# Prompt attention of a hybrid decoder step: normalization moved behind the value products

## The reference

```python
s = einsum('bqgrd,bngd->bqgrn', q, ck) * scale - slopes * dist_c
p = softmax(where(vm, s, NEG)) * vm
o_cmp = einsum('bqgrn,bngd->bqgrd', p, cv)
...
s2 = einsum('bqgrd,bqgnd->bqgrn', q, ks) * scale - slopes * dist_s
p2 = softmax(where(m2, s2, NEG))
o_slc = einsum('bqgrn,bqgnd->bqgrd', p2, vs)
# o_win: the same with the window branch's keys and values
g = sigmoid(gates)
o = g[..., 0:1] * o_cmp + g[..., 1:2] * o_slc + g[..., 2:3] * o_win
```

## Time and profile before

| | |
|---|---|
| three runs, us | 3301.79, 3307.1, 3315.38 (median 3307.1) |
| the profiled execution, span | 3315.7 us |
| PE busy | 3062.8 us (92%) |
| DVE busy | 2161.3 us (65%) |
| ACT busy | 1199.0 us (36%) |
| POOL busy | 522.0 us (16%) |

### The profile page before, as it was taken

The page is one execution under the profiler, slowest core; times in us unless marked ns, Lnnn a source line. Parts: engine busy times, 40 slices in busy tenths (PEclk is TensorE's granted clock), DMA queues, the critical chain, the costliest instruction groups (busy, mean ns, idle before and its releaser), DMA issues.

```text
span 3315.7 us, 57097 instructions
## 1 busy us (share of the span) xinstructions
PE 3062.8 (92%) x23903; PEld 2911.4 (88%) x23903; DVE 2161.3 (65%) x3361; ACT 1199.0 (36%) x2108; POOL 522.0 (16%) x294
## 2 busy tenths in 40 slices
PE   7999999997988877999898899999999999999995
PEld 7999988996867655788897899999999999999995
DVE  3111777815645444366556888888888889888887
ACT  2000333104634332244223444444444444444342
POOL 2333332433460020011232000000000000000000
PEclk6999999998999987899998999999999999999997
DMA  6744245418812166022633434444444447344332
GB/s 195 224 123 126 70 131 156 139 52 279 282 66 110 71 249 190 17 89 83 169 87 93 140 116 123 122 122 123 125 126 126 126 126 237 120 144 162 97 111 105
DMA packets 517928, 443.70 MB, mean 134 GB/s; under 512 B 33168, under 2 KB 469552, under 8 KB 510750
## 3 DMA queue, kind: packets, MB, share of 16 engines
q1 hardware_dynamic: 453608, 306.83, 31.8%
q0 software_dynamic: 17488, 75.78, 6.1%
q10 hardware_dynamic: 46576, 57.44, 5.1%
HBM read 377.39 MB, written 70.93 MB: 135 GB/s over the span
## 4 chain that ended last, share of the span: by engine, by line
PE 43%; DVE 6%; DMA 1%; issue 1%; ACT 1%; ACTq 0%; DVEq 0%; SPq 0%
PE i L2537 37%; PE i L129 6%; DMA x_blocks<-s_blk 1%; DVE x_blocks L3041 1%; DVE f_half L3003 1%; DVE y_rows L3113 0%; DVE ln_parts L3047 0%; DVE y_rows L3118 0%; DVE resid L2902 0%; ACT x_blocks L2818 0%; DVE x_blocks L2916 0%; DMA x_rows<-s_h 0%; PE i L2546 0%; DVE m_lo L2849 0%; DVE h_rows L3036 0%
## 5 line engine op out<-in xcount | busy, mean ns | idle before, releaser
L2537 PE MATMUL i<-x_blocks,f_half 128*128 128x272 f32 x10752 | 1368.2, 289 | 36.6 <-DVE h_rows L3036 13.7
L2537 PEld LDWEIGHTS i<-x_blocks,f_half 128*128 128x128 f32 x10752 | 1359.4, 190 | 41.3 <-DVE x_blocks L3041 16.0
L2752 ACT CAST f_half<-w_ring 128x1024 fp32r<-128x1024 f32 (+2 forms) x370 | 346.2, 936 | 408.2 <-PE i L2537 355.5
L3003 DVE TENSOR_TENSOR f_half<-w_ring,f_half 128x1024 fp32r<-128x1024 f32 (+2 forms) x362 | 393.1, 1086 | 81.2 <-ACT f_half L2752 78.4
L129 PE MATMUL a<-x_hi,w_hi 128*128 128x272 f32 x1664 | 349.5, 291 | 18.3 <-POOL w_lo L545 18.3
L129 PE MATMUL a<-x_hi,w_lo 128*128 128x272 f32 x1664 | 345.9, 289 | 0.0
L129 PE MATMUL a<-x_lo,w_hi 128*128 128x272 f32 x1664 | 344.8, 289 | 0.0
L545 POOL TENSOR_TENSOR w_lo<-w_ring,w_hi 128x2048 fp32r<-128x2048 f32 x52 | 240.8, 4631 | 455.6 <-DVE w_hi L553 455.6
L129 PEld LDWEIGHTS a<-x_hi,w_hi 128*128 128x128 f32 x1664 | 263.5, 189 | 23.7 <-POOL w_lo L545 23.0
L129 PEld LDWEIGHTS a<-x_lo,w_hi 128*128 128x128 f32 x1664 | 263.2, 190 | 0.0
L553 DVE CAST w_hi<-w_ring 128x2048 fp32r<-128x2048 f32 x52 | 70.7, 1362 | 293.7 <-PE a L129 293.7
(11 more groups left out here) (498 smaller groups left out, 4585.8 us busy)
## 6 DMA issues: line engine op xcount, KB each, us to landing
w_ring<-in_ffn_w_up_dram SPq DMA_DIRECT2D x88, 1024.0 KB, 10.6
w_ring<-in_w_in_dram SPq DMA_DIRECT2D x52, 1024.0 KB, 6.9
w_ring<-in_ffn_w_down_dram SPq DMA_DIRECT2D x24, 1536.0 KB, 7.9
w_ring<-in_w_o_dram SPq DMA_DIRECT2D x16, 1024.0 KB, 6.0
x_blocks<-s_blk ACTq DMA_DIRECT2D x17, 816.0 KB, 5.8
s_blk<-x_sums ACTq DMA_DIRECT2D x22, 544.0 KB, 6.8
s_proj<-x_nat ACTq DMA_DIRECT2D x40, 272.0 KB, 2.6
kv_ring<-in_cmp_w_dram SPq DMA_DIRECT2D x16, 512.0 KB, 11.6
```

The lines of the kernel that those rows point to most:

```text
L2537: last = nc.tensor.matmul(ps[bank][:, 0:HT2], half(e, j, wl_)[:, s], XB[:, x0 + s, xl_, BLK_OF[j]], start=start and s == 0 and i == 0, sto ...
L2752: nc.scalar.copy(half(e, j, 0), source(e, j)).then_inc(hq, 1)
L3003: nc.vector.tensor_tensor(half(e, j, 1), source(e, j), half(e, j, 0).bitcast(F32), ALU.subtract).then_inc(lv, 1)
```

## The change

The softmax weights are no longer normalized before the value products. `turn` transposes the bare exponentials with the identity as operand (a plain transpose, one record), and `values` exchanges its operands, so that the queries stand on the partitions of the result; the three branches go to three separate column ranges of the bank. DVE then combines them (`combine`): reciprocal of the sums, times the gates, and three 128x128 steps that read the bank and add the branches with their factors. The row result is transposed back by PE (`out_turn`), and ACT copies it to `mix` for each job.

The compressed branch of all heads is done once, in front: 32 small score products, bias, shift by the maximum, one exponential, normalization, four transposes. Its weights lie on 64 partitions (8 heads x 8 blocks), and the compressed values `CVX` are laid out so that a head's product picks its own rows (other heads' rows are zero). For this the stage before makes the hidden rows for four heads (`HIDX`, four activations) and one masked 64x1024 product on DVE. All queries are loaded at once to `MIX` in the stage before, in place of two heads there and six loads in the attention; each head's result then overwrites its queries.

The core of the diff:

```diff
-                for h in range(2):
-                    sp.dma_start(Q[:, h], S_proj[h * P:(h + 1) * P, 0:SEQ]).then_inc(q_in[h], 16)
+                sp.dma_start(MIX[:, 0:H, 0:SEQ], S_proj[0:H * P, 0:SEQ].rearrange("(h p) n -> p h n", p=P)).then_inc(q_in, 16)
...
-                nc.vector.tensor_copy(CVP[:].rearrange("p g d -> p (g d)"), ps[2][0:NPB, 0:KVH * HD]).then_inc(ckv, 1)
+                dve.wait_ge(kv_in, 144)
+                nc.vector.tensor_tensor(CVX, ps[2][0:H * NPB, 0:HD].rearrange("p (o d) -> p o d", o=1).broadcast_to((H * NPB, H, HD)),
+                                        OWN.rearrange("p (h o) -> p h o", o=1).broadcast_to((H * NPB, H, HD)), ALU.mult).then_inc(ckv, 1)
...
+                def compressed_scores():
+                    for t in range(QT):
+                        for h in range(H):
+                            at = (t * H + h) * NPB
+                            last = nc.tensor.matmul(pso[1][:, at:at + NPB], MIX[:, h, t * P:(t + 1) * P], CKP[:, :, h // GRP], start=True, stop=True)
+                    last.then_inc(c_scores, 1)
...
                     for br in range(2):
-                        u = UNITS[j] + br
-                        pe.wait_ge(d_ready, u + 1)
+                        u = 2 * j + br
+                        pe.wait_ge(e_ready, u + 1)
                         if u >= 2:
                             pe.wait_ge(pts_ready, u - 1)
                         for k in range(qt + 1):
-                            last = nc.tensor.matmul(pst[u % 2][:, k * P:(k + 1) * P], SC[:, j % 3, br, k * P:(k + 1) * P], DG[:, j % 2, br],
-                                                    start=True, stop=True)
+                            last = nc.tensor.transpose(pst[u % 2][:, k * P:(k + 1) * P], SC[:, j % 3, br, k * P:(k + 1) * P], ident)
...
-                    nc.tensor.matmul(o, CVP[:, g], PTC[:, h % 2, qt * P:(qt + 1) * P], start=True, stop=False)
+                    nc.tensor.matmul(o[:, 0:HD], PTC[:, qt * P:(qt + 1) * P], CVX[:, h], start=True, stop=True)
                     for br in range(2):
-                        pe.wait_ge(pts_ready, UNITS[j] + br + 1)
+                        pe.wait_ge(pts_ready, 2 * j + br + 1)
                         for k in range(qt + 1):
-                            last = nc.tensor.matmul(o, V[:, k, br, g], PTS[:, j % 2, br, k * P:(k + 1) * P], start=False, stop=br == 1 and k == qt)
+                            last = nc.tensor.matmul(o[:, (br + 1) * HD:(br + 2) * HD], PTS[:, j % 2, br, k * P:(k + 1) * P], V[:, k, br, h // GRP],
+                                                    start=k == 0, stop=k == qt)
...
+                def out_turn(j):
+                    pe.wait_ge(r_ready, j + 1)
+                    nc.tensor.transpose(pso[j % 2][:, 0:HD], OR[:, j % 2], ident).then_inc(ot_done, 1)
...
                 scores(1)
+                compressed_scores()
                 for j in range(NJ):
                     turn(j)
                     if j + 2 < NJ:
                         scores(j + 2)
+                    if j == 1:
+                        compressed_turn()
                     if j:
                         values(j - 1)
+                    if j >= 2:
+                        out_turn(j - 2)
...
+                def combine(j):
                     h, qt = JOBS[j]
+                    o, r, to = pso[j % 2], RI[:, j % 2], OR[:, j % 2]
+                    dve.wait_ge(e_ready, 2 * j + 2)
+                    ch.link(nc.vector.reciprocal(r, SU[:, j % 4]))
+                    ch.link(nc.vector.tensor_tensor(r, r, GAB[:, qt, 3 * h + 1:3 * h + 3], ALU.mult))
+                    dve.wait_ge(o_done, j + 1)
+                    if j >= 2:
+                        dve.wait_ge(ot_done, j - 1)
+                    ch.link(nc.vector.tensor_scalar(to, o[:, HD:2 * HD], r[:, 0:1], None, ALU.mult))
+                    ch.link(nc.vector.scalar_tensor_tensor(to, o[:, 2 * HD:3 * HD], r[:, 1:2], to, ALU.mult, ALU.add))
+                    nc.vector.tensor_tensor(to, o[:, 0:HD], to, ALU.add).then_inc(r_ready, 1)
```

More of the change, by code:

```diff
@@ L47 @@
 BIG = 1e33
+NPB_ = SEQ // BLK
 R_Q, R_KV, R_QKV = 0, O_KV, O_GATE
@@ L705, in build @@
         kv_in = sem("a_kv_in")
-        q_in = [sem(f"a_q_in{i}") for i in range(2)]
+        q_in = sem("a_q_in")
         att = ExitStack()
@@ L827, in _ @@
                 nc.tensor.matmul(ps[0][:, :], W2[:, 0], HID[:, 0], start=True, stop=True).then_inc(out4, 1)
[L828 to L831, removed]
+                nc.tensor.matmul(ps[1][:, 0:2 * NPB], W2[:, 0], HIDP[:], start=True, stop=True).then_inc(out4, 1)
+                nc.tensor.matmul(ps[2][0:H * NPB, 0:HD], HIDX[:].rearrange("p g r n -> p (g r n)"), W2[:, 1], start=True, stop=True).then_inc(out4, 1)
                 for k in range(4):
@@ L862, in _ @@
                 act.wait_ge(pc, 1)
-                for c in range(2):
-                    nc.scalar.activation(HIDP[:, c], ps[6 + c][:, 256:256 + 2 * NPB], ACT.Silu).then_inc(hid, 1)
+                nc.scalar.activation(HIDP[:], ps[6][:, 256:256 + 2 * NPB], ACT.Silu).then_inc(hid, 1)
+                for r in range(GRP):
+                    last = nc.scalar.activation(HIDX[:, :, r], ps[7][:, 256:256 + 2 * NPB].rearrange("p (n g) -> p g n", g=KVH), ACT.Silu)
+                last.then_inc(hid, 1)
             @block.vector
@@ L1060, in _ @@
                         scores(j + 2)
+                    if j == 1:
+                        compressed_turn()
                     if j:
                         values(j - 1)
+                    if j >= 2:
+                        out_turn(j - 2)
                 values(NJ - 1)
+                for j in range(NJ - 2, NJ):
+                    out_turn(j)
             @block.scalar
@@ L1093, in output @@
                     h, qt = JOBS[j]
-                    if qt == QT - 1:
-                        act.wait_ge(o_done, QT * (h + 1))
-                        nc.scalar.copy(MIX[:, h, 0:SEQ], pso[h % 2][:, :]).then_inc(o_out, 1)
+                    act.wait_ge(ot_done, j + 1)
+                    nc.scalar.copy(MIX[:, h, qt * P:(qt + 1) * P], pso[j % 2][:, 0:HD]).then_inc(o_out, 1)
                 for j in range(NJ):
                     expo(j)
+                    if j == 0:
+                        act.wait_ge(c_shift, 1)
+                        c = SCC[:].rearrange("p t h n -> p (t h n)")
+                        nc.scalar.activation(c, c, ACT.Exp).then_inc(c_exp, 1)
                     if j >= 1:
                         turned(j - 1)
+                    if j == 1:
+                        act.wait_ge(c_turned, 1)
+                        nc.scalar.copy(PTC[:], pso[0][0:H * NPB, :]).then_inc(c_ready, 1)
                     if j >= 3:
                         output(j - 3)
+                output(NJ - 3)
                 turned(NJ - 1)
-                output(NJ - 3)
-                output(NJ - 2)
-                output(NJ - 1)
+                for j in range(NJ - 2, NJ):
+                    output(j)
             @block.vector
@@ L1112, in _, with by_block, compressed_bias @@
                 ch = Count(dve, ch5)
[L1114 to L1117 removed]
+                def by_block(x):
+                    return x.rearrange("p t (h o) -> p t h o", o=1).broadcast_to((P, QT, H, NPB))
+                def compressed_bias():
+                    for h in range(H):
+                        last = nc.vector.tensor_scalar(BC[:, :, h], cp("dist_c").rearrange("p (t n) -> p t n", t=QT), cp("slope")[:, h:h + 1], None, ALU.mult)
+                    ch.link(last)
```

160 lines of the change are left out of this document (65 added, 95 removed).

## The result

| | before | after |
|---|---|---|
| runs, us | 3301.79, 3307.1, 3313.75, 3315.38 | 3270.86, 3272.02, 3277.91, 3282.89 |
| median, us | 3310.43 | 3274.97 |
| profiled execution, span, us | 3315.7 | 3276.0 |
| attention stage in it, us | 173.75 | 138.82 |
| one head in it, us | 19.87 | 14.74 |

The changed kernel is faster by 1%: ratio 0.9897, interval 0.9879 to 0.9915. The forecast of 3277 is 2 us from the median. The stage, from PE's first product of the attention to its first one of the next stage, lost 34.9 us where 30.2 were forecast.

What follows compares the result with a forecast made beforehand. PE's waits for DVE's diagonal matrices in a multi-engine loop were taken as the bound. Stage: 0.4 + 9.5 + 8 x 15.4 + 3.5, plus 7.0 for the long head, 143.6 against 173.8 us, -30: 3277 us, range 3262 to 3295.

Steps and rivals of the forecast that it cites:

- PE's work in a head: PE's products and transposes for one attention head: 17.41 us before, 14.9 after, bounds 14.1 to 16.9.
- The loop: Tightest at the four-key-tile job: 4.6 us from scores to turn, PE busy 4.05, waiting 0.5; a head 15.4 us.
- The output of job a: DVE's combination for the one-key-tile job: done at 3.9 us, PE arrives at 3.65 to 3.85; nothing counted.
- DVE: DVE's combination costs 1.4 us a job; 12.5 us of work in a head of 15.4, so it hides.
- The front: Start of the attention stage, compressed scores of all heads first: costs 9.5 us, bounds 8 and 9.5 + 5.
- The tail: Last values, combination, transpose and copy of the final job behind the loop: 3.5 us over a whole head.
- The long head: One attention head, coinciding with the gather of the sample group's rows, stays 7.0 us longer than usual.
- The rival in which it vanishes: The 7.0 us stall of one attention head falls elsewhere or on nothing: another -7, 3270 us; chance 0.25.
- Neighbours: Stage before the attention: about +0.4 us from extra activations; the 2 MB query load nothing, at most +3.
- Turns that don't get cheaper: Rival: a transpose in the turns costs 0.23 us like a product, 16.9 us a head, 3289 us; chance 0.07.
- DVE as the bound: Rival: DVE sets the head at 16.6 to 17.2 us, 12 us more, 3289 us; chance 0.08.
- the fallen clock in the loop: Rival: attention stage stays at 1.2 GHz through front pauses and transposes, 98 us more, 3375 us; chance 0.03.

Runs made afterwards that it cites:

- the kernels built from the one before: Kernel before, normalization left out: plain transposes with the diagonal wait kept, 3300.55 us; identity products without that wait, 3288.98; transposes without it, 3271.3.
- the doubled step: Changed kernel with the first of DVE's three output steps of each job made twice: 3275.61 us, heads of 14.74.
- the kernel with all three edits: Changed kernel with 128-row compressed value product, job 1 ahead of the compressed branch in front, ACT's copies ahead of exponentials: 3260.53 us, ratio 0.9868.
- three close relatives of it: Changed kernel with ACT's copies ahead of exponentials, 3273.72 us; with job 1 ahead of the compressed branch, 3261.8; with both and 128-row compressed value products, 3260.53.
- the first kernel: Changed kernel with the turns as full products with the identity in place of plain transposes: 3291.38 us, heads of 16.38.
- the third form of the kernel before: Kernel before without diagonals and normalization, turns as plain transposes waiting for the exponentials alone: 3271.3 us, heads of 15.40.
- the last edits: Changed kernel with ACT's copies ahead of the exponentials, 3273.72 us; with that, 128-row compressed value products and job 1 first in front, 3260.53.

## Why the prediction was right, point by point

- *PE's work in a head* was forecast as 14.9, and a wait of 0.5 beside it. Measured are 14.26 and 0.48 (by starts 13.89 and 0.85). The term that was mis-sized is the transpose: 0.131 from the busy time of 48 in another stage, where eight take 0.91, start to start, 0.113 each. Twenty make 0.36 us less. The output transposes are 0.11, not 0.2, another 0.36. Together they are nearly the difference of a head, 15.4 to 14.74: 0.66 x 8 = 5.3 us of the stage.
- *The loop.* The place (job d), the partner (ACT), and the chain (4.64 against 4.6) came as laid out. That the wait has the forecast size (0.48 against 0.5) is in part luck: it is two waits, 0.31 for ACT and 0.17 for DVE, and by starts PE is late by 0.85, since it needs 3.79 us beside the chain and not 4.05. The output of job a, called tight, is late by 0.17 and costs nothing, as counted, since that time lies beside the chain.
- *Wait and transposes apart.* "Turns now wait for ACT's exponentials and no diagonals" is worth 2.7 us a head and the transposes 1.8, by the kernels built from the one before.
- *DVE* needs 1.45 us a job for the five steps of the combination (1052.38 to 1053.83), forecast 1.4. It hides, as the doubled step shows, even at a busy share of 88%; but the room at job a is only some 0.5 us (0.38 and 0.15), and the kernel with all three edits has used it up.
- *The front* costs 11.16 us (22.07 to the first turn of d, less 10.91 for the same piece of a steady head), forecast 9.5. The step that failed is "All compressed scores come first: 8 x 0.88 = 7.0 us": they took 8.7, since the clock fell to 0.50 before they ended. The prediction took the fall of the earlier trace rows for the result of idle time and expected the load to prevent it; PE was busy 5.00 of 5 us and the mean clock was 0.67. All eight kernels that make these scores first had the clock fall during them.
- *The tail* costs 4.66 against 3.5: its last value product, combination and transpose stand one behind the other with waits of 0.36, 1.10 and 0.90 us.
- *The long head* shrank to 5.14 where 7.0 were kept. Of the 1.9, 1.0 is a shorter pause (3.5 against 4.5) and 0.9 a shorter stretch at the low clock behind it. The rival in which it vanishes did not occur in the changed kernel, but in three close relatives of it, if those can be compared (see above): it is better priced as a spread of 0 to 7 us than as a case of its own.
- *Neighbours.* The stage started 0.26 us later (forecast 0.4), and the query load of 2 MB cost nothing.
- *The sum:* 11.16 + 8 x 14.74 + 5.14 + 4.66 = 138.9, and 138.82 is measured. The forecast counted from the same start 143.2. Its errors of +1.7 in the front, -5.3 in the heads, -1.9 in the long head and +1.2 in the tail make -4.3. That the whole time came within 2 us is in part luck. The forecast took 30.2 from 3307.1, the median of three runs; with the fourth run that median is 3310.43, and the gain is 35.5. An error of 3.3 in the one and of 5.3 in the other nearly cancel. In the profiled executions the span lost 39.7 us, 34.9 of it in this stage, 2.3 in the sample attention behind it (270.95 against 273.2), and the rest is spread.
- *The rivals.* Turns that don't get cheaper, DVE as the bound, and the fallen clock in the loop are excluded by the first kernel, the doubled step and the clock of 1.00. The clock was the nearest to coming true: in the third form of the kernel before it fell in some heads.

The 8 heads of the stage thus explain the change: 5.11 us each, 40.9 us, less 7.9 us that front and tail cost more than before, and 1.9 that the long head gives back.

## What to carry over

Lay the loop out as two parts: the main engine's own work on one side, and the chain of its partners on the other. A head was 10.10 + 4.64 here. That foretold the heads of the last edits (14.24 in 14.1 to 14.3, 13.46 in 13.3 to 13.7) and accounts afterwards for those of the earlier ones; two of their expectations had added work that runs beside the chain and is free. Moving a normalization behind a product takes it out of that chain even when it makes DVE busier, from 51 to 78%, and does no harm until DVE itself is late at one place of the loop, which the busy share doesn't show. Time work by starts, not by busy time, and look at the granted clock of a stretch before you price anything in it.

## What the runs showed of the hardware

- **The clock fell while PE was busy.** 32 products of 8 columns (64 records, 8.72 us) ran without a gap, and the granted clock went from 1.00 to 0.50 in them, in all eight kernels that have them. In the loop, transposes followed by four such products brought it to 0.50 in three heads of two kernels, and either one without the other did not in the steady part.
- **A product with 64 rows between products with 128** takes 0.41 us instead of 0.22, and its neighbours 0.1 more each. Zeros in the other 64 rows paid: 0.78 us a head.
- **A transpose of a 128x128 f32 tile** takes 0.113 us start to start, a product 0.23.
- **DVE and ACT can pause together, and PE behind them.** It was seen only with the gather running, in one head, which got 2.7 to 7.0 us longer by it and by a lower clock behind it, and in three kernels with the gather not at all. What they wait for stays open.
